# The up projection of a streaming encoder step made token-major, with 512 weight columns streamed

## The chip, the cores and the metric

The kernel runs on one core of a Trainium2 chip. The metric is device time of one execution in microseconds (us). TensorE does the matmuls, VectorE, ScalarE and GpSimd the elementwise work. SyncE, ScalarE and GpSimd issue DMAs.

## The reference, cut to what matters

One layer over 400 tokens: 16 meta tokens and 256 new frames of one stream, and 16 new frames of each of 8 running streams. Attention and mLSTM heads come first, then an output projection, then a squared-ReLU MLP, all in fp32. The meta tokens' MLP output is not wanted, so the MLP sees 384 tokens. What matters here:

```python
def merge_and_ffn(x, att, hm, og, mnorm_g, w_out, norm2_g, w_up, w_down):
    ...
    x = x + mix @ w_out                              # D_MODEL = 2048
    u = jax.nn.relu(rms_norm(x, norm2_g) @ w_up)     # D_FF = 8192
    return x + jnp.square(u) @ w_down
```

## The kernel before, in words

Each fp32 matmul is made of three on TensorE in the float32r format: both factors are split into a high part and a low part (the rest), and high x high, high x low and low x high are summed in PSUM. So each tile of weights is loaded into `raw` by SyncE, split by ScalarE into `w_hi` (`split_hi`, L494) and by VectorE into `w_lo` (`split_lo`, L503), and used. A tile is a pair of loads of 512 KB and has four quarters of 128x512. `w_hi` and `w_lo` hold four quarters: ScalarE may split a quarter of the next tile once TensorE is done with the same quarter of this one (`w_used`). ScalarE and VectorE thus run one tile ahead of TensorE, in an order that is written out in each engine's program. Every other operation of theirs stands between two splits of that order.

The MLP runs in four groups of 2048 features (`GROUPS`), each group an up stage of 16 tiles and a down stage of 16 tiles.

In the up stage the weights are stationary: a tile holds 2048 rows by 128 columns of `w_up`, and the 384 tokens (`x2g_hi`, `x2g_lo`, features on partitions) stream past (`mm_tile`, L523 to L525, 48 matmuls of 384 columns). The result in `acc[j]` has 128 features on its partitions and tokens in its columns. VectorE multiplies it by the norm's factor, which has been spread over all partitions beforehand (L1882 to L1885, `spread_rstd`), into `n_t` (L1894), and takes ReLU times itself into `n_sq` (L1898). ScalarE makes its high part `a_hi` (L1243), GpSimd its low part `a_lo` (L846).

In the down stage the activations are stationary: for each of four blocks of 512 columns, 16 k and three groups of 128 tokens, `a_hi`/`a_lo` [128 features, 128 tokens] are loaded and 512 columns of `w_down` stream past (`mm_down`, L623 to L625) into three PSUM banks. VectorE adds them to `y_rows` (L1917). The two sets of three banks take turns (`down_banks`).

Ahead of the MLP, the second half of the output projection (`mm_out`) ends each of four column blocks of the residual x2, which is token-major in `y_rows`. The first two blocks are turned to feature-major by VectorE's 32x32 block transpose (L1644), 12 stores from GpSimd that put the blocks in place in device memory, and one load (the helper at L657). The last eight tiles are turned by TensorE (L2214) into PSUM banks that `x2_bank` names. ScalarE also issues 32 stores of new keys earlier on (L1079), and SyncE loads the key cache in 128-byte pieces (L905).

## Time and profile before

| | |
|---|---|
| median of 3 runs | 1751.79 us (1751.28 to 1752.92) |
| the profiled execution | 1751.83 us |
| its span | 1750.0 us |
| TensorE busy | 1743.2 us |
| VectorE, ScalarE, GpSimd busy | 902.0, 670.9, 224.1 us |
| weight loads of w_up | 128 of 512 KB, 4.0 us to landing |
| weight loads of w_down | 128 of 512 KB, 3.7 us to landing |

The span is the time between the first and the last instruction of the profiled execution. Busy times overlap between engines. A matmul's recorded duration overlaps that of the next one, so TensorE's pace is read from the distance between starts.

### The profile page before, as it was taken

The numbers are of one execution on the slowest core, as the hardware profiler recorded it, in microseconds if no ns is written. First come the engines' busy times: TensorE is split into PE (matmuls) and PEld (weight loads), VectorE is DVE, ScalarE is ACT, GpSimd is POOL, SyncE is SP. The second block draws the span as 40 slices with busy tenths as digits, with TensorE's granted clock in tenths as the row PEclk, the third lists the DMA queues.
The fourth block names the chain that finished last, engine by engine and source line by source line (L and its number), as shares of the span: only waits on it lengthen the run. The fifth ranks groups of instructions, "written<-read, shape, count | busy, mean of one in ns | idle before, by whom it ended". The sixth has DMA issues, their size and how long they took to land.

```text
span 1750.0 us, 27145 instructions
## 1 busy us (share of the span) xinstructions
PE 1743.2 (100%) x9246; PEld 1581.0 (90%) x9246; DVE 902.0 (52%) x1724; ACT 670.9 (38%) x1256; POOL 224.1 (13%) x312
## 2 busy tenths in 40 slices
PE   9999999999999999999999999999999999999999
PEld 8999998889997789998889999888999888999887
DVE  5634776666677656554344444344454334545333
ACT  5323754444354444333333333333333333333332
POOL 3301010002351250110000110000111000111000
PEclk9999999999999999999999999999999999999999
DMA  7675469998788584444334443334443334444443
GB/s 187 186 181 150 122 169 223 204 203 215 201 259 258 147 210 123 129 122 126 127 123 129 120 125 126 124 128 121 130 121 125 126 123 130 120 127 125 142 147 97
DMA packets 382545, 264.69 MB, mean 151 GB/s; under 512 B 92860, under 2 KB 328572, under 8 KB 382476
## 3 DMA queue, kind: packets, MB, share of 16 engines
q1 hardware_dynamic: 353190, 222.09, 45.1%
q0 software_dynamic: 14224, 37.83, 8.2%
q10 hardware_dynamic: 15062, 3.86, 1.1%
q8 instruction: 42, 0.69, 0.2%
q14 instruction: 27, 0.22, 0.0%
HBM read 246.47 MB, written 23.03 MB: 154 GB/s over the span
## 4 chain that ended last, share of the span: by engine, by line
PE 98%; DVE 1%; issue 0%; ACT 0%; POOL 0%; POOLq 0%; DVEq 0%; ACTq 0%
PE acc L523 18%; PE acc L524 18%; PE acc L525 18%; PE bank L624 9%; PE bank L625 8%; PE bank L623 8%; PE bank L1940 3%; PE ssb L623 2%; PE ssb L624 2%; PE ssb L625 2%; PE ssb L1940 1%; PE bank L569 1%; PE bank L570 1%; PE bank L568 1%; PE acc L568 1%; PE acc L570 1%
## 5 line engine op out<-in xcount | busy, mean ns | idle before, releaser
L503 DVE TENSOR_TENSOR w_lo<-raw,w_hi 128x512 fp32r<-128x512 f32 x768 | 556.4, 733 | 769.2 <-ACT w_hi L494 768.3
L494 ACT ACTIVATE w_hi<-raw 128x512 fp32r<-128x512 f32 x768 | 483.5, 632 | 821.1 <-PE acc L525 400.2
L524 PE MATMUL acc<-x2g_lo,w_hi 128*128 128x384 f32 x1024 | 348.0, 340 | 0.0
L523 PE MATMUL acc<-x2g_hi,w_hi 128*128 128x384 f32 x1024 | 345.9, 338 | 0.0
L525 PE MATMUL acc<-x2g_hi,w_lo 128*128 128x384 f32 x1024 | 344.6, 337 | 0.0
L523 PE MATMUL acc<-a_hi,w_hi 128*128 128x400 f32 (+1 forms) x768 | 268.1, 349 | 0.2 <-DVE w_lo L503 0.2
L524 PE MATMUL acc<-a_lo,w_hi 128*128 128x400 f32 (+1 forms) x768 | 262.9, 342 | 0.0
L525 PE MATMUL acc<-a_hi,w_lo 128*128 128x400 f32 (+1 forms) x768 | 262.3, 342 | 0.0
L624 PE MATMUL bank<-w_lo,a_hi 128*128 128x512 f32 x640 | 253.0, 395 | 0.0
L625 PE MATMUL bank<-w_hi,a_lo 128*128 128x512 f32 x640 | 252.6, 395 | 0.0
L623 PE MATMUL bank<-w_hi,a_hi 128*128 128x512 f32 x640 | 252.0, 394 | 0.0
L525 PEld LDWEIGHTS acc<-x2g_hi,w_lo 128*128 128x128 f32 x1024 | 193.4, 189 | 0.0
L524 PEld LDWEIGHTS acc<-x2g_lo,w_hi 128*128 128x128 f32 x1024 | 192.4, 188 | 0.1
L523 PEld LDWEIGHTS acc<-x2g_hi,w_hi 128*128 128x128 f32 x1024 | 191.9, 187 | 0.5 <-DVE w_lo L503 0.3
L846 POOL TENSOR_TENSOR a_lo<-n_sq,a_hi 128x384 f32 x64 | 65.2, 1018 | 899.4 <-ACT a_hi L1243 899.4
L523 PEld LDWEIGHTS acc<-a_hi,w_hi 128*128 128x128 f32 x768 | 144.2, 188 | 6.5 <-issue 4.0
L625 PEld LDWEIGHTS bank<-w_hi,a_lo 128*128 128x128 f32 x640 | 120.7, 189 | 27.7
L624 PEld LDWEIGHTS bank<-w_lo,a_hi 128*128 128x128 f32 x640 | 120.3, 188 | 27.8
L623 PEld LDWEIGHTS bank<-w_hi,a_hi 128*128 128x128 f32 x640 | 120.4, 188 | 27.6
L525 PEld LDWEIGHTS acc<-a_hi,w_lo 128*128 128x128 f32 x768 | 144.8, 189 | 0.0
L524 PEld LDWEIGHTS acc<-a_lo,w_hi 128*128 128x128 f32 x768 | 144.3, 188 | 0.3
L1243 ACT ACTIVATE a_hi<-n_sq 128x384 f32 (+1 forms) x64 | 33.7, 527 | 131.9 <-DVE n_sq L1898 131.9
(344 smaller groups left out, 1533.9 us busy)
## 6 DMA issues: line engine op xcount, KB each, us to landing
raw<-in_w_up SPq DMA_DIRECT2D x128, 512.0 KB, 4.0
raw<-in_w_down SPq DMA_DIRECT2D x128, 512.0 KB, 3.7
raw<-in_w_in SPq DMA_DIRECT2D x94, 512.0 KB, 4.7
raw<-in_w_out SPq DMA_DIRECT2D x32, 512.0 KB, 4.9
vc<-in_cache_v POOLq DMA_DIRECT2D x32, 256.0 KB, 7.3
kc<-in_cache_k SPq DMA_DIRECT2D x128, 64.0 KB, 3.2
state_blocks<-in_state_C POOLq DMA_DIRECT2D x16, 256.0 KB, 4.5
C_blk<-state_blocks SPq DMA_DIRECT2D x4, 1024.0 KB, 8.5
```

What stands on the lines that cost most here:

```text
L494: e.activation(w_hi[:, q], raw[:, slot, 4 * (q % 2):4 * (q % 2) + 4, :], ACT.Copy).then_inc(hi_ready, 1)
L503: e.tensor_tensor(w_lo[:, q], raw[:, slot, 4 * (q % 2):4 * (q % 2) + 4, :], w_hi[:, q].bitcast(F32), ALU.subtract).then_inc(lo_ready, 1)
L523: e.matmul(out, w_hi[:, q, kk], hi[:, k, at], start=k == 0, stop=False, skip_group_check=True)
L524: e.matmul(out, w_hi[:, q, kk], lo[:, k, at], start=False, stop=False, skip_group_check=True)
L525: last = e.matmul(out, w_lo[:, q, kk], hi[:, k, at], start=False, stop=k == KT - 1, skip_group_check=True)
L568: e.matmul(out, a_hi[:, k, rows], hi_w, start=k % 8 == 0, stop=False, skip_group_check=True)
L570: last = e.matmul(out, a_lo[:, k, rows], hi_w, start=False, stop=k % 8 == 7, skip_group_check=True)
L623: e.matmul(out, a_hi[:, k, rows], hi_w, start=k == 0, stop=False, skip_group_check=True)
L624: e.matmul(out, a_hi[:, k, rows], lo_w, start=False, stop=False, skip_group_check=True)
L625: last = e.matmul(out, a_lo[:, k, rows], hi_w, start=False, stop=k == KT - 1, skip_group_check=True)
L846: e.tensor_tensor(a_lo[:, bass.ds(2 * i + j, 1), LIVE], n_sq[:, j:j + 1, LIVE], a_hi[:, bass.ds(2 * i + j, 1), LIVE].bitcast(F32), ALU.sub ...
L1940: return e.matmul(out, lhsT, rhs, start=start, stop=stop, skip_group_check=True)
```

## The change

The up projection takes down's form. For each group there are four blocks (`U_BLOCKS`) of 512 features. The normed tokens are stationary (128 at a time) and 512 columns of `w_up` stream past (`mm_up`), into the same `down_banks` in turn. SyncE loads `w_up` as it loads `w_down`, in rows of 512 columns.

The result is now token-major, and the down stage wants it with features on partitions. For each block: VectorE scales by the norm's factor, one number per partition now, and takes ReLU from PSUM into `u_rows` (`turn_u`, three operations of 128x512). ScalarE squares in place (`square_u`, three). VectorE transposes within 32x32 blocks into `u_blk` (three). ScalarE issues 12 stores of 64 KB that put the blocks in their places in device memory (`store_u`). GpSimd loads the turned block of 512 features into `u_land` (`u_part`). ScalarE makes its high part (`u_hi`, four), GpSimd its low part (four). In ScalarE's order the squares stand behind the last split of the block (fourth tile's turn), the stores behind the first split of the next block's first turn, the high parts behind the first split of its third turn; behind a group's last block these turns are those of the down stage's first block. In all there are 16 blocks.

The spreading of the norm's factor over the partitions is gone. The x2 tiles 8 to 15 that TensorE turns go into `acc` (8 to 11, 15) and the second set of down banks (12 to 14), since the first set is now up's. The semaphore `y_summed` is renamed `rows_summed` and `x2_landed` `rows_landed`, with the counts moved to suit.

```diff
@@ -189,6 +189,7 @@
 Y_STARTS = (NPR, META, META + P)
 Y_TURNS = (1, 2, 0)
 X2_BLOCKS = 2
+U_BLOCKS = 4
 Y_OUT = 2 * len(Y_PLAN)
 Y_OUT_SUMMED = 2 * 2 * 4
 LAST_IN_BANK = [("nout")] + [(x, *y, NH - 1) for x, y in (("num", (0,)), ("num", (1,)), ("num", (2,)), ("cp", ()),
@@ -290,6 +291,7 @@
         gate_rows = nc.dram_tensor("gate_rows", [3, NH, TOK], F32).ap()
         new_keys = nc.dram_tensor("new_keys", [4, 8, 13 * 32, 32], F32).ap()
         x2_turned_d = nc.dram_tensor("x2_turned", [X2_BLOCKS, 4 * P, 3 * P], F32).ap()
+        u_turned_d = nc.dram_tensor("u_turned", [2, 4 * P, 3 * P], F32).ap()
         state_blocks_d = nc.dram_tensor("state_blocks", [P, BD * NH, DV], F32).ap()
@@ -592,9 +594,56 @@
                     (T_OUT2 + 7, 1): (8, 9), (T_OUT2 + 7, 3): (10, 11)}.get((t, q), ())
         def x2_bank(k):
-            if k == KT - 1:
-                return bank[1]
-            return down_banks[k // 4 % 2][k % 4 % 3]
+            if k < 12 or k == KT - 1:
+                return acc[k % 2 if k < 12 else 0]
+            return down_banks[1][k % 4]
+        u_rows, u_blk = (m1[:].rearrange("p j t -> p (j t)")[:, 12 * P * x:12 * P * (x + 1)].rearrange("p (r n) -> p r n", r=3)
+                         for x in range(2))
+        u_land = stage[:].rearrange("p j t -> p (j t)")[:, 0:12 * P].rearrange("p (k t) -> p k t", k=4)
+        def u_store(e, g, b, r):
+            for a in range(4):
+                e.dma_start(bass.AP(tensor=u_turned_d.tensor,
+                                    offset=(b % 2) * 4 * P * 3 * P + Y_STARTS[r] - META + 32 * a,
+                                    ap=[[3 * P, 32], [32 * 3 * P, 16], [1, 32]]),
+                            u_blk[32 * a:32 * a + 32, r]).then_inc(S("u_stored"), 16)
+        def mm_up(e, g, b, first=False, after=None):
+            out = down_banks[b % 2]
+            def products(kq, q, r):
+                k = 4 * kq + q
+                if k == 0:
+                    if b < 2:
+                        e.wait_ge(S("y_added"), 12 * g + (Y_OUT - 6 + 3 * b + r + 1))
+                    else:
+                        e.wait_ge(S("u_read"), 12 * g + (3 * (b - 2) + r + 1))
+                hi_w, lo_w = (w[:, q].rearrange("p k n -> p (k n)") for w in (w_hi, w_lo))
+                to, rows = out[r][:], slice(Y_STARTS[r], Y_STARTS[r] + P)
+                e.matmul(to, x2g_hi[:, k, rows], hi_w, start=k == 0, stop=False, skip_group_check=True)
+                e.matmul(to, x2g_hi[:, k, rows], lo_w, start=False, stop=False, skip_group_check=True)
+                last = e.matmul(to, x2g_lo[:, k, rows], hi_w, start=False, stop=k == KT - 1, skip_group_check=True)
+                if k == KT - 1 and r < 2:
+                    last.then_inc(S("rows_summed"), 1)
+                if r == 2:
+                    last.then_inc(w_used, 1)
+            for kq in range(4):
+                pair, j = g * KT + (T_MLP // 2 + 2 * b + kq // 2), kq % 2
+                for qs in ((0,), (1,), (2, 3)) if kq == 3 else ((0,), (1,), (2,), (3,)):
+                    e.wait_ge(lo_ready, 8 * pair + 4 * j + qs[-1] + 1)
+                    if first:
+                        e.wait_ge(S("x2_lo_made"), 4 * kq + qs[-1] + 1)
+                    for r in range(3):
+                        for q in qs:
+                            products(kq, q, r)
+                    if after and kq == 0:
+                        for q in qs:
+                            after(q)
         x2_blocks = stage[:].rearrange("p j t -> p (j t)")[:, 0:3 * 4 * P]
...
-            e.memset(st4[:, 5], 0.0).then_inc(S("u_lo_made"), 1)
-            e.memset(st4[:, 4], 0.0).then_inc(S("u_lo_made"), 1)
-            with e.Fori(0, GROUPS) as g:
-                with e.Fori(0, KT // 2) as i:
-                    for j in range(2):
-                        e.wait_ge(S("u_hi_made"), KT * g + 2 * i + j + 1)
-                        e.tensor_tensor(a_lo[:, bass.ds(2 * i + j, 1), LIVE], n_sq[:, j:j + 1, LIVE],
-                                        a_hi[:, bass.ds(2 * i + j, 1), LIVE].bitcast(F32),
-                                        ALU.subtract).then_inc(S("u_lo_made"), 1)
+                    "rows_landed")
+            def u_part(g, b, first=False):
+                n = U_BLOCKS * g + b
+                e.wait_ge(S("u_stored"), 192 * n + 192)
+                if not first:
+                    e.wait_ge(S("u_lo_made"), 4 * n)
+                e.dma_start(u_land, u_turned_d[b % 2].rearrange("(k p) t -> p k t", p=P)).then_inc(S("rows_landed"), 16)
+                for k in range(4):
+                    e.wait_ge(S("u_hi_made"), KT * g + (4 * b + k + 1))
+                    e.tensor_tensor(a_lo[:, 4 * b + k, LIVE], u_land[:, k], a_hi[:, 4 * b + k, LIVE].bitcast(F32),
+                                    ALU.subtract).then_inc(S("u_lo_made"), 1)
+            for g in range(GROUPS):
+                for b in range(U_BLOCKS):
+                    u_part(g, b, first=g == b == 0)
             for n, (r, c) in enumerate(Y_PLAN[:-3]):
                 e.wait_ge(S("y_added"), Y_OUT + 12 * (GROUPS - 1) + n + 1)
@@ -941,9 +997,10 @@
                 if T_OUT + 2 <= t < T_OUT + 6:
                     load_x(t - T_OUT - 2)
             with e.Fori(0, GROUPS) as g:
-                with e.Fori(0, KT // 2) as i:
-                    for j in range(2):
-                        load_tile(e, g * KT + i + T_MLP // 2, j, w_up[0], 0, g * D + i * (2 * P) + P * j)
+                with e.Fori(0, U_BLOCKS) as c:
+                    for kq in range(4):
+                        load_rows(e, g * KT + 2 * c + (T_MLP // 2 + kq // 2), kq % 2, w_up[0],
+                                  kq * 4 * P, g * D + c * (4 * P))
                 with e.Fori(0, 4) as c:
                     for kq in range(4):
                         load_rows(e, g * KT + 2 * c + (T_MLP // 2 + KT // 2 + kq // 2), kq % 2, w_down[0],
@@ -1231,34 +1288,56 @@
                     e.wait_ge(S("y_logged"), 1)
                     e.activation(y_st[:, 4], y_st[:, 3], ACT.Exp, scale=-0.5).then_inc(S("y_rooted"), 1)
-            def split_up(g, first=False):
-                e.wait_ge(w_used, 4 * PER_GROUP * g + 4 * T_MLP)
-                def pair(i, after):
-                    for j in range(2):
-                        split_hi(e, g * KT + i + (T_MLP // 2 + j), 1 - j, after=after if j == 0 else None)
-                        e.wait_ge(S("u_made"), KT * g + 2 * i + j + 1)
-                        at = bass.ds(2 * i + j, 1)
-                        e.activation(a_hi[:, at, LIVE], n_sq[:, j:j + 1, LIVE], ACT.Copy).then_inc(S("u_hi_made"), 1)
-                if first:
-                    pair(0, first_up)
-                with e.Fori(1 if first else 0, KT // 2) as i:
-                    pair(i, None)
+            def square_u(g, b):
+                for r in range(3):
+                    e.wait_ge(S("u_read"), 12 * g + (3 * b + r + 1))
+                    e.activation(u_rows[:, r], u_rows[:, r], ACT.Square).then_inc(S("u_squared"), 1)
+            def store_u(g, b):
+                for r in range(3):
+                    e.wait_ge(S("u_blocks"), 12 * g + (3 * b + r + 1))
+                    u_store(e, g, b, r)
+            def u_hi(g, b):
+                e.wait_ge(S("rows_landed"), 16 * (U_BLOCKS * g + b) + 16 * (X2_BLOCKS + 1))
+                for k in range(4):
+                    e.activation(a_hi[:, 4 * b + k, LIVE], u_land[:, k], ACT.Copy).then_inc(S("u_hi_made"), 1)
+            def up_block(g, b, first=False):
+                for kq in range(4):
+                    def after(q):
+                        if first and kq == 0:
+                            first_up(q)
+                        if b and (kq, q) == (0, 0):
+                            store_u(g, b - 1)
+                        elif b and (kq, q) == (2, 0):
+                            u_hi(g, b - 1)
+                        elif b < U_BLOCKS and (kq, q) == (3, 3):
+                            square_u(g, b)
+                    split_hi(e, g * KT + (T_MLP // 2 + 2 * b + (kq + 1) // 2), (kq + 1) % 2, after=after)
             def split_down(g):
-                with e.Fori(0, KT // 2) as i:
+                up_block(g, U_BLOCKS)
+                with e.Fori(2, KT // 2) as i:
                     for j in range(2):
                         split_hi(e, g * KT + i + (T_MLP // 2 + KT // 2 + j), 1 - j)
+            def split_up(g, first=False):
+                for b in range(U_BLOCKS):
+                    up_block(g, b, first=first and b == 0)
             split_up(0, first=True)
             split_down(0)
-            with e.Fori(1, GROUPS - 1) as g:
+            for g in range(1, GROUPS - 1):
                 split_up(g)
                 split_down(g)
             split_up(GROUPS - 1)
-            with e.Fori((T_END - KT) // 2, T_END // 2 - 1) as p:
+            up_block(GROUPS - 1, U_BLOCKS)
+            with e.Fori((T_END - KT) // 2 + 2, T_END // 2 - 1) as p:
                 for j in range(2):
                     split_hi(e, p + j, 1 - j)
             split_hi(e, T_END // 2 - 1, 1)
@@ -1878,30 +1957,32 @@
                     y_step(tt(y_st[:, 5], y_st[:, 5], y_st[:, 2], ALU.mult), 4)
                     y_step(ts(y_st[:, 5], y_st[:, 5], -0.5, 1.5, ALU.mult, ALU.add), 5)
                     y_step(tt(y_st[:, 6], y_st[:, 5], y_st[:, 4], ALU.mult), 6)
-                    for r in range(3):
-                        last = ts(n_y[:, 0, r * P:(r + 1) * P], ident[:], y_st[:, 6, r:r + 1], None, ALU.mult)
-                    last.then_inc(S("y_diag_made"), 1)
-                    e.wait_ge(S("rstd2_spread"), 1)
-                    e.tensor_copy(rstd_x[:, LIVE], bank[0][:, LIVE]).then_inc(S("rstd2_ready"), 1)
-                    e.wait_ge(S("rstd2_ready"), 1)
+            def turn_u(g, b):
+                n = U_BLOCKS * g + b
+                for r in range(3):
+                    if r < 2:
+                        e.wait_ge(S("rows_summed"), 16 * g + (Y_OUT_SUMMED + 2 * b + r + 1))
+                    else:
+                        tile_done(e, g * KT + (T_MLP // 2 + 2 * b + 1), 1)
+                    ts(u_rows[:, r], down_banks[b % 2][r][:], y_st[:, 6, r:r + 1], 0.0, ALU.mult,
+                       ALU.max).then_inc(S("u_read"), 1)
+                for r in range(3):
+                    e.wait_ge(S("u_squared"), 12 * g + (3 * b + r + 1))
+                    if r == 0 and not (isinstance(n, int) and n == 0):
+                        e.wait_ge(S("rows_landed"), 16 * n + 16 * X2_BLOCKS)
+                    e.transpose(u_blk[:, r], u_rows[:, r]).then_inc(S("u_blocks"), 1)
             def up(g, first=False):
-                def pair(i, after):
-                    for j in range(2):
-                        t = KT * g + 2 * i + j
-                        split_lo(e, g * KT + i + (T_MLP // 2 + j), 1 - j, after=after if j == 0 else None)
-                        tile_done(e, g * KT + i + T_MLP // 2, j)
-                        tt(n_t[:, LIVE], acc[j][:, LIVE], rstd_x[:, LIVE], ALU.mult).then_inc(acc_free, 1)
-                        e.wait_ge(acc_free, KT * g + 2 * i + (T_OUT + j + 1))
-                        e.wait_ge(S("u_lo_made"), t + 1)
-                        stt(n_sq[:, j, LIVE], n_t[:, LIVE], 0.0, n_t[:, LIVE], ALU.max,
-                            ALU.mult).then_inc(S("u_made"), 1)
-                if first:
-                    pair(0, first_up)
-                with e.Fori(1 if first else 0, KT // 2) as i:
-                    pair(i, None)
+                for b in range(U_BLOCKS):
+                    for kq in range(4):
+                        def after(q):
+                            if first and b == 0 and kq == 0:
+                                first_up(q)
+                            if (kq, q) == (3, 3):
+                                turn_u(g, b)
+                        split_lo(e, g * KT + (T_MLP // 2 + 2 * b + (kq + 1) // 2), (kq + 1) % 2, after=after)
             def down(g, c2, half, last):
                 for kq in range(4):
...
@@ -2218,35 +2299,20 @@
             for t in range(T_OUT2, T_MLP):
                 mm_out(e, t, after=new_x)
-            def spread_rstd(q):
-                if q == 1:
-                    e.wait_ge(S("y_diag_made"), 1)
-                    for r in range(3):
-                        last = mm(bank[0][:, Y_STARTS[r]:Y_STARTS[r] + P], ones[:], n_y[:, 0, r * P:(r + 1) * P], True, True)
-                    last.then_inc(S("rstd2_spread"), 1)
-            x2_there = lambda k: e.wait_ge(S("x2_lo_made"), k + 1)
-            def up_pair(g, i, afters=(None, None), first=False):
-                for j in range(2):
-                    mm_tile(e, g * KT + i + T_MLP // 2, j, x2g_hi, x2g_lo, each=x2_there if first and j == 0 else None,
-                            at=LIVE, after=afters[j], used=KT * g + 2 * i + (T_OUT + j))
             def down_all(g):
                 with e.Fori(0, 2) as c2:
                     for half in range(2):
                         mm_down(e, g, c2, half)
-            up_pair(0, 0, (lambda q: new_x(T_MLP, q), spread_rstd), first=True)
-            with e.Fori(1, KT // 2) as i:
-                up_pair(0, i)
+            for b in range(U_BLOCKS):
+                mm_up(e, 0, b, first=b == 0, after=(lambda q: new_x(T_MLP, q)) if b == 0 else None)
             down_all(0)
             with e.Fori(1, GROUPS - 1) as g:
-                with e.Fori(0, KT // 2) as i:
-                    up_pair(g, i)
+                for b in range(U_BLOCKS):
+                    mm_up(e, g, b)
                 down_all(g)
-            with e.Fori(0, KT // 2) as i:
-                up_pair(GROUPS - 1, i)
+            for b in range(U_BLOCKS):
+                mm_up(e, GROUPS - 1, b)
             for c2 in range(2):
                 for half in range(2):
                     mm_down(e, GROUPS - 1, c2, half, tail=c2 == 1 and half == 1)
```

## Rows read from the trace of the kernel before

**Rows 1.** The page's chain that ended last, share of the span by engine.

```profile
PE 98%; DVE 1%; issue 0%; ACT 0%; POOL 0%; POOLq 0%; DVEq 0%; ACTq 0%
```

**Rows 2.** Busy time by stretch: start:end us, busy us by engine, PEclk, DMA share, GB/s.

```profile
940.20:1075.20 135.00, 135.00 (x769) 135.00 (x767) 67.81 (x97) 47.48 (x79) 15.29 (x15) 1.00 0.42 124
1075.20:1208.90 133.70, 133.70 (x578) 108.58 (x578) 50.83 (x75) 41.03 (x65) 1.02 (x1) 1.00 0.39 125
```

**Rows 3.** Waits from 640 on, ScalarE's and SyncE's: us in all, times, longest.

```profile
ACT w_hi L494 <- PE acc L525: 225.6, 193, 1.5
...
SPq L471 <- DVE w_lo L503: 451.9, 128, 6.6
```

**Rows 4.** TensorE's timeline (start us, us, instruction), first matmul of six stages.

```profile
669.01 0.42 PE L523 MATMUL acc<-x2g_hi,w_hi 128*128 128x384 f32 x1
...
806.58 0.39 PE L623 MATMUL bank<-w_hi,a_hi 128*128 128x512 f32 x1
...
940.12 0.34 PE L523 MATMUL acc<-x2g_hi,w_hi 128*128 128x384 f32 x1
...
1075.37 0.39 PE L623 MATMUL bank<-w_hi,a_hi 128*128 128x512 f32 x1
...
1208.90 0.34 PE L523 MATMUL acc<-x2g_hi,w_hi 128*128 128x384 f32 x1
...
1344.15 0.39 PE L623 MATMUL bank<-w_hi,a_hi 128*128 128x512 f32 x1
```

**Rows 5.** TensorE's timeline, turns of x2 tiles in the first up tile.

```profile
673.31 0.82 PE L2214 MATMUL bank<-ident,y_rows 128*128 128x128 f32 x6
673.96 0.49 PE L2214 MATMUL ssb<-ident,y_rows 128*128 128x128 f32 x3
```

**Rows 6.** Timeline of ScalarE and VectorE behind the border at 1344.15.

```profile
1344.41 0.63 ACT L494 ACTIVATE w_hi<-raw 128x512 fp32r<-128x512 f32 x1 [1.54 <-PE acc L525]
...
1345.08 0.69 DVE L503 TENSOR_TENSOR w_lo<-raw,w_hi 128x512 fp32r<-128x512 f32 x1 [1.48 <-ACT w_hi L494]
1345.69 0.55 DVE L1894 TENSOR_TENSOR n_t<-acc,rstd_x 128x384 f32<-128x384 f32 x1
```

**Rows 7.** Timeline of VectorE and ScalarE, operations of one kind in a row.

```profile
619.25 1.88 DVE L1631 TENSOR_TENSOR y_rows<-bank,y_rows 128x512 f32<-128x512 f32 x3
621.26 1.90 DVE L1644 STREAM_TRANSPOSE stage<-y_rows 128x512 f32<-128x512 f32 x3
...
686.15 1.66 ACT L494 ACTIVATE w_hi<-raw 128x512 fp32r<-128x512 f32 x3
```

**Rows 8.** Timeline of DMA issues (q), ScalarE's first and last at the start among them.

```profile
253.24 0.35 ACTq L1079 DMA_DIRECT2D new_keys<-ko  x1
253.69 0.64 ACT L494 ACTIVATE w_hi<-raw 128x512 fp32r<-128x512 f32 x1 [2.88 <-DVE ko L1564]
...
0.78 0.42 ACTq L964 DMA_DIRECT2D g_rows<-in_norm_g  x1
...
6.27 0.88 ACTq L969 DMA_DIRECT2D xn<-in_x_prompt  x1
...
249.91 6.06 SPq L905 DMA_DIRECT2D kc<-in_cache_k  x8
```

**Rows 9.** All stores of line 1079: ns of an issue (min/median/max), landing.

```profile
L1079 ACTq DMA_DIRECT2D new_keys<-ko x32: 309/310/1100, 253.2 to 338.4; - x32
...
DMA to landing us min/median/max: 2.0/4.2/10.0
```

**Rows 10.** Timeline of GpSimd and ScalarE, second x2 block through device memory.

```profile
640.12 7.74 POOL L657 DMA_DIRECT2D x_turned<-stage  x12 [4.60 <-DVE stage L1644]
652.16 0.78 POOL L657 DMA_DIRECT2D m<-x_turned  x1 [4.29 <-DMA x_turned<-stage]
...
657.24 1.13 ACT L1215 ACTIVATE x2g_hi<-m,g 128x384 fp32r<-128x384 f32 x2 [0.38 <-DMA m<-x_turned]
```

**Rows 11.** The page's costliest groups: busy us, mean ns, idle before.

```profile
L846 POOL TENSOR_TENSOR a_lo<-n_sq,a_hi 128x384 f32 x64 | 65.2, 1018 | 899.4 <-ACT a_hi L1243 899.4
```

More of the change, by code:

```diff
@@ L571, in products @@
                 if k % 8 == 7 and r < 2:
-                    last.then_inc(S("y_summed"), 1)
+                    last.then_inc(S("rows_summed"), 1)
                 if r == 2:
@@ new lines, in u_store @@
+        def u_store(e, g, b, r):
[19 more added lines that the diff above has]
+                if k == KT - 1 and r < 2:
+                    last.then_inc(S("rows_summed"), 1)
+                if r == 2:
[12 more added lines that the diff above has]
+                            after(q)
@@ L609, in x2_there_for @@
             if k < 4 * X2_BLOCKS:
-                e.wait_ge(S("x2_landed"), 16 * (k // 4 + 1))
+                e.wait_ge(S("rows_landed"), 16 * (k // 4 + 1))
             else:
@@ L620, in products @@
                     e.wait_ge(S("y_added"), 12 * g + 6 * c2 + (Y_OUT - 6 + 3 * half + r + 1))
+                    e.wait_ge(S("u_read"), 12 * g + (6 + 3 * half + r + 1))
                 hi_w, lo_w = (w[:, q].rearrange("p k n -> p (k n)") for w in (w_hi, w_lo))
@@ L626, in products @@
                 if k == KT - 1 and r < 2:
-                    last.then_inc(S("y_summed"), 1)
+                    last.then_inc(S("rows_summed"), 1)
                 if r == 2:
@@ L634, in mm_down @@
                     e.wait_ge(lo_ready, 8 * pair + 4 * j + qs[-1] + 1)
-                    e.wait_ge(S("u_lo_made"), KT * g + (4 * kq + qs[-1] + 3))
+                    e.wait_ge(S("u_lo_made"), KT * g + (4 * kq + qs[-1] + 1))
                     for r in range(3):
@@ L837, in _ @@
                 dma(m1[:, 4 * c:4 * c + 4, 0:3 * P], x2_turned_d[c].rearrange("(k p) t -> p k t", p=P),
-                    "x2_landed")
-            e.memset(st4[:, 5], 0.0).then_inc(S("u_lo_made"), 1)
-            e.memset(st4[:, 4], 0.0).then_inc(S("u_lo_made"), 1)
-            with e.Fori(0, GROUPS) as g:
-                with e.Fori(0, KT // 2) as i:
-                    for j in range(2):
-                        e.wait_ge(S("u_hi_made"), KT * g + 2 * i + j + 1)
-                        e.tensor_tensor(a_lo[:, bass.ds(2 * i + j, 1), LIVE], n_sq[:, j:j + 1, LIVE],
-                                        a_hi[:, bass.ds(2 * i + j, 1), LIVE].bitcast(F32),
-                                        ALU.subtract).then_inc(S("u_lo_made"), 1)
+                    "rows_landed")
[12 more added lines that the diff above has]
+                    u_part(g, b, first=g == b == 0)
             for n, (r, c) in enumerate(Y_PLAN[:-3]):
@@ L1626, in add_out @@
                     if r < 2:
-                        e.wait_ge(S("y_summed"), 2 * (4 * half + c) + r + 1)
+                        e.wait_ge(S("rows_summed"), 2 * (4 * half + c) + r + 1)
                     else:
@@ L1912, in down @@
                     if r < 2:
-                        e.wait_ge(S("y_summed"), 8 * g + 4 * c2 + (Y_OUT_SUMMED + 2 * half + r + 1))
+                        e.wait_ge(S("rows_summed"), 16 * g + 4 * c2 + (Y_OUT_SUMMED + 8 + 2 * half + r + 1))
                     else:
@@ L2210, in new_x @@
                     e.wait_ge(S("y_added"), Y_OUT // 2 + 3 * (k // 4) + 3)
-                    if k % 4 == 3:
-                        e.wait_ge(S("x2_lo_made"), k - 2 if k < KT - 1 else 12)
+                    if k in (10, 11, KT - 1):
+                        e.wait_ge(S("x2_lo_made"), k - 1 if k < KT - 1 else 11)
                     for r in range(3):
```

## The prediction

> **What bounds the kernel now.** I read the chain of waits first, then the busy times in stretches, then TensorE's timeline at the borders of the stages. TensorE holds 98% of the chain [rows 1]: only what TensorE does, or waits for, moves the end. In the two stages of the MLP (up projection, then down projection, four groups of each) it never pauses, and the granted clock is 1.00, its upper level of 2.4 GHz [rows 2]. Its weight loads are busy for all 135.00 us of an up stage, but for 108.58 of 133.70 in a down stage. ScalarE and VectorE are ahead of TensorE by design: ScalarE waits 225.6 us in all for TensorE to give back a quarter of `w_hi`, and SyncE waits 451.9 us for a free `raw` buffer before it may issue an up load [rows 3]. So the weight traffic has slack, and the question for the change is the pace of TensorE's new instructions on one side, and whether ScalarE and VectorE stay ahead on the other.
>
> **TensorE's pace.** A whole up stage runs from 940.12 to 1075.37, 135.25 us for 768 matmuls of 384 columns (0.1761 from start to start) [rows 4]. The down stage behind it runs to 1208.90, 133.53 us for 576 matmuls of 512 columns (0.2318). The changed up stage has 4 blocks x 16 k x 3 row groups x 3 products = 576 matmuls of down's form: the same columns in fewer instructions. I take down's 133.53 us for it: 1.72 us less in each of three groups, 5.2 us (the other two groups repeat the pair of intervals to 0.01 us). Group 0 lasts from 669.01 to 806.58, 137.57 us. In it stay the twelve turns of the last x2 tiles, of which six took 673.96 - 673.31 = 0.65 us [rows 5], so 1.3 for twelve; what goes is the spreading of the norm's factor over all partitions (three fp32 products, three VectorE scalings, a copy). 137.57 - 133.53 - 1.3 = 2.7 us. TensorE's part is -7.9 us. Where no engine falls behind, the span is 1742.1. Bounds of this term: without the group 0 part -5.2, and down's pace is measured, so not much beyond -8.
>
> The Trainium skill, TensorE: Matmul & The Clock Gate, section "Back-to-back issue gap", gives an isolated warm gap of N/2.4 + 2.5 ns. As an estimate by that formula 3072 x 162.5 ns against 2304 x 215.8 ns would save 2.0 us over the four groups, where the trace's own paces save 6.9 (5.2 plus 1.7 in group 0): rows decide.
>
> **Work that lies beside it.** Down's blocks have 64 quarters, 133.53/64 = 2.09 us each; one tile of four quarters is 8.35 us, and a block of four tiles 33.4 us. Per up block VectorE gets 3 scalings from PSUM and 3 block transposes of 128x512, ScalarE 3 squares and 4 copies, GpSimd one load and 4 subtractions. Before, four 128-feature tiles cost VectorE eight operations and ScalarE four copies; the sums of both engines (67.8 and 47.5 of 135 us, [rows 2]) leave room. What matters is when they come, since `w_hi` and `w_lo` hold one tile of four quarters and every split is queued behind them.
>
> I set t = 0 at the start of TensorE's first matmul of the next block, and take the border at 1344.15 [rows 4]. ScalarE's last split of the finished block's turn starts at 0.26, VectorE's at 0.93, and VectorE is free at 1.54 [rows 6]. The three scalings start at 1.54, 2.14, 2.74 (three adds from PSUM took 1.88 together, each 0.60 behind the last, [rows 7]). The squares follow each at once: from 2.26, 2.90 and 3.46. ScalarE's split of quarter 0 of the next tile follows at 4.0, 0.53 behind the last square (three splits in 1.66, [rows 7]). The transposes start at 3.34 and follow 0.62 apart (three in 1.90, [rows 7]); the first is ready at 4.01, the third at 5.24. TensorE needs quarter 0 at 8.35, and VectorE does its low part right behind the transposes, by 6: covered.
>
> **The twelve stores are not covered.** Behind quarter 0 ScalarE's queue issues the block's 12 stores (3 row groups x 4 partition groups, 64 KB each in 512 pieces of 128 bytes), and only then splits quarter 1. ScalarE does not compute past a DMA that it issues: the issue at 253.24 took 0.35, and the activation behind it starts at 253.69, 0.10 after it ended [rows 8]. With p us from one issue to the next, they run from 4.05 to 4.05 + 12p. Then come 0.10, and the 1.36 us from the start of a split to the end of its low part (1344.41 to 1345.77, [rows 6]). TensorE wants that quarter at 8.35 + 2.09 = 10.43. So it stops for s = 4.05 + 12p + 1.46 - 10.43 = 12p - 4.92 us in each block, and the point from which the stores cost anything is p = 0.41.
>
> What is p? A lone store of nearly this form from ScalarE (52 KB in 128-byte pieces) took 0.31, median of 32 [rows 9]. Behind one another they have no row on this queue in this form. The nearest: ScalarE's 11 loads at the start run from 0.78 to 7.15, 0.58 each; SyncE's loads of 64 KB in 128-byte pieces, the same count of pieces, took 6.06 us for 8, 0.76 each, behind weight loads in their own queue [rows 8]. The ends are 0.31 (s = 0) and 0.76 (s = 4.2). I take 0.58, the one row of back-to-back issues on ScalarE's own queue, where no weight load is ahead; s = 2.0 us. There are 16 blocks, the last of each group too, whose stores fall into the down stage: +32.6 us. Behind the stop ScalarE catches up at once, 0.53 per split against 2.09 per quarter, so each block pays once.
>
> In a sentence apart: the Trainium skill, DMA: Bandwidth & Descriptors, section "Issuing engines are not separate DMA queues", says that the time to start a DMA on a sequencer is "usually small relative to the DMA itself". Applied here it speaks for the lone-store row of 0.31 and for no stop, the first rival below. The trace agrees that it is small beside a landing (0.31 against 4.2, [rows 9]), but small is not free when 12 stand in one row.
>
> **The way through device memory.** Last issue at 4.05 + 7.0 = 11.0. In the stage before the MLP the same twelve pieces from GpSimd's queue were issued until 647.86, the load of them began at 652.16 (4.30 later), its issue took 0.78, and its data was used at 657.24, 4.3 after that [rows 10]. Here: 11.0 + 4.3 + 0.8 + 4.3 = 20.4. ScalarE asks for it behind the split of quarter 0 of the fourth tile, which TensorE frees at 2 x 8.35 + 2.09 + s + 0.26 = 21.1: no wait. After the four copies (taken as 0.53 each, like the splits) and 1.46 as above, quarter 1 must be ready by 3 x 8.35 + 2.09 + s = 29.2, so the landing may come as late as 29.2 - 2.1 - 1.46 = 25.6, 5.2 later than worked out. The low parts (4 x 1.02 on GpSimd, [rows 11]) are needed from tile 4 of down's first block, at 25.0 + s; the first is there by 23.2: hidden by the three tiles ahead of them. Each block's traffic (0.79 MB out in 6144 pieces, 0.79 MB back) goes into DMA engines that are 39 to 42% busy [rows 2], and the up loads change to 2 KB pieces like down's: no cost taken for either.
>
> The renamed semaphores, the new PSUM buffers for x2 tiles 8 to 15 and their waits, and the reading waits of the down banks come long after their releases (TensorE turned the x2 tiles into idle banks at 673.31 without a pause behind them, [rows 5]): nothing, and a few tenths once if wrong. The tail is not touched.
>
> **Sum.** 1750.0 - 7.9 + 32.6 = 1774.7 span. The profiled execution took 1751.83 for a span of 1750.0, so 1.8 lies around it, and it stands 0.04 from the median of 1751.79: 1776.5 us.
>
> **Rivals.**
> *Issues stay cheap.* p below 0.41, no stop: 1742.1 + 1.8 = 1743.9, faster by 0.45%. For it: 0.31 per lone store, and this queue is empty when the stores begin. Against it: every run of issues in the trace, on both queues, is above 0.41 on average.
> *Both effects nearly cancel.* p of 0.43 to 0.49, a stop of 0.2 to 1.0: 1748 to 1759, the lower half within the bound. For it: the shorter ones among ScalarE's first issues (0.42, [rows 8]).
> *The landing is the late one.* If the stores, sharing the 16 engines with the weight stream, need the worst landing of a store from this queue (10.0 instead of 4.2, [rows 9]), the data comes at 26.2 and costs 0.6 more per block, 1786; if the load is late by as much again, it comes at 32.0 and costs 6.4 more per block, 1879. Against it: the x2 case ran in a busier stretch. It decides from a landing 5.2 us later than mine.
> *A deeper stop.* p at or above SyncE's 0.76: s of 4.2 or more, 1811 and up.
>
> **Chances.** Forecast (p of 0.50 to 0.76, 1761 to 1811, its own range) 0.60; cheap issues 0.20; cancelling 0.09; late landing 0.06; deeper stop 0.05. What a measurement tells from no change is about 0.2%, 3.5 us. Faster: the cheap case and a part of the cancelling one, 0.23. Same 0.07, slower 0.70. The range reaches from the cheap case to the top of the forecast's own, 1744 to 1811.
>
> **What would show it.** Right: 576 matmuls per up stage 0.232 apart; a TensorE pause in quarter 1 of the second tile behind every up block, ended by VectorE's low part behind ScalarE's split, with ScalarE idle before that split for the length of 12 issues; nothing lost at the fourth tile. Wrong: issues of 0.35 in a row and a chain with no pause (first rival); ScalarE waiting on the landed data with TensorE stopped near the fourth tile (third); a granted clock below 1.00 behind the pauses, which would make every matmul after them dearer; or up matmuls that don't keep down's pace.

## The result, and the profile after

The changed kernel takes 1782.15 us (median of 6 runs, 1780.23 to 1783.34), the one before 1752.09 (6 runs, 1751.28 to 1752.92): a ratio of 1.0171, 95% interval [1.0158, 1.0184], so 1.7% slower. The profiled execution took 1781.35 us with a span of 1779.2. Forecast were 1776.5 us and slower.

The page's first line on busy time and its chain by engine, of the kernel after:

```profile
PE 1742.8 (98%) x8472; PEld 1474.4 (83%) x8472; DVE 875.1 (49%) x1688; ACT 688.6 (39%) x1304; POOL 242.4 (14%) x326
...
PE 87%; ACTq 5%; DVE 4%; ACT 2%; issue 2%; DMA 0%; DVEq 0%
```

Against [rows 1] TensorE's share of the chain falls from 98 to 87%, and ScalarE's queue (ACTq), which was at 0, holds 5%: DMA issues are now on the path that sets the end. The DVE, ACT and issue shares belong to the same stretches, as the chain walks back over the late split, the squares and the scalings.

The busy times by stretch of the kernel after, one row for the up stage of group 1 and one for the down stage behind it (columns as in [rows 2], the stretch cut at the stages' first matmuls):

```profile
946.80:1088.50 141.70, 135.57 (x577) 109.23 (x576) 58.13 (x84) 49.20 (x85) 15.74 (x15) 0.99 0.54 152
1088.50:1224.30 135.80, 134.03 (x577) 108.17 (x577) 54.35 (x80) 43.75 (x73) 5.26 (x5) 1.00 0.45 137
```

The up stage has down's 576 matmuls and its weight loads are busy for 109 us of it instead of 135, but it takes 141.7 us instead of 135.0, and TensorE is busy for 135.57 of them. The down stage takes 2.1 us more than before: the last block's stores fall into it.

One block border in time, group 1, ScalarE's timeline (start, us, engine, line, times, idle before). TensorE's first matmul of the new block starts at 980.10.

```profile
979.67 1.33 ACT L496 ACTIVATE w_hi<-raw 128x512 fp32r<-128x512 f32 x2 [2.84 <-PE bank L629]
982.42 1.95 ACT L1295 ACTIVATE m<-m 128x512 f32<-128x512 f32 x3 [1.42 <-DVE m L1969]
984.27 0.62 ACT L496 ACTIVATE w_hi<-raw 128x512 fp32r<-128x512 f32 x1
984.35 6.41 ACTq L608 DMA_DIRECT2D u_turned<-m  x12
990.86 2.19 ACT L496 ACTIVATE w_hi<-raw 128x512 fp32r<-128x512 f32 x4 [5.97 <-PE ssb L629]
```

The squares (L1295), the split of quarter 0, twelve issues that take 6.41 us, and only then the splits that had been due. The "5.97 <-PE" is an example of a wait put down to the wrong one: TensorE had given the quarter back at about 984.5, and what ended at 990.76 was the last issue. VectorE's and then TensorE's timeline of the same stretch:

```profile
981.64 2.06 DVE L1969 TENSOR_SCALAR m<-bank,y_st 128x512 f32<-128x512 f32 x3
983.62 1.88 DVE L1975 STREAM_TRANSPOSE m<-m 128x512 f32<-128x512 f32 x3
...
991.52 1.90 DVE L505 TENSOR_TENSOR w_lo<-raw,w_hi 128x512 fp32r<-128x512 f32 x3 [5.44 <-ACT w_hi L496]
```

```profile
990.29 0.39 PE L629 MATMUL ssb<-w_hi,x2g_lo 128*128 128x512 f32 x1
992.27 0.50 PE L627 MATMUL bank<-w_hi,x2g_hi 128*128 128x512 f32 x1 [1.59 <-DVE w_lo L505]
992.60 0.39 PE L628 MATMUL bank<-w_lo,x2g_hi 128*128 128x512 f32 x1
```

From 990.29 to 992.27 are 1.98 us where 0.23 is the pace: a stop of 1.75 us. The matmul after that starts 0.33 later and not 0.23; behind each of the other stops it is the same. There are 16 such stops, one per block. By the starts of the matmuls on both sides they come to 31.8 us: twelve of 1.68 to 1.89, and 2.12, 2.64, 2.74 and 2.95. The view of waits (us in all, times, longest) has them as 12 in up and 4 in down:

```profile
PE bank L627 <- DVE w_lo L505: 22.9, 12, 2.8
PE bank L673 <- DVE w_lo L505: 6.3, 4, 1.6
```

(It counts from the recorded end of the matmul before, which lies 0.16 us into the pause, so 29.2 and not 31.8.)

The stores and the load of the turned block, page of the kernel after, section on DMA issues (us to landing last), and the stores' line (ns of one issue, min/median/max):

```profile
u_turned<-m ACTq DMA_DIRECT2D x192, 64.0 KB, 1.9
stage<-u_turned POOLq DMA_DIRECT2D x16, 768.0 KB, 6.8
```

```profile
L608 ACTq DMA_DIRECT2D u_turned<-m x192: 309/522/1528, 707.4 to 1650.3; - x192
```

### The profile page after: what moved, and what is told of

It is laid out like the page before. It is cut to its first block, busy times and chain, and to the rows that moved or that the text cites. A ratio compares the mean times of both kernels' runs of the same rounds, so it can differ in the third digit from the quotient of the medians.

```text
span 1779.2 us, 24776 instructions
## 1 busy us (share of the span) xinstructions
PE 1742.8 (98%) x8472; PEld 1474.4 (83%) x8472; DVE 875.1 (49%) x1688; ACT 688.6 (39%) x1304; POOL 242.4 (14%) x326
## 4 chain that ended last, share of the span: by engine, by line
PE 87%; ACTq 5%; DVE 4%; ACT 2%; issue 2%; DMA 0%; DVEq 0%
PE bank L673 8%; PE bank L674 8%; PE bank L675 8%; PE acc L525 8%; PE acc L526 8%; PE acc L527 8%; PE bank L627 7%; PE bank L628 6%; PE bank L629 6%; ACTq L608 5%; PE bank L2021 3%; ACT w_hi L496 2%; PE ssb L673 2%; PE ssb L674 2%; PE ssb L675 2%
## 5 line engine op out<-in xcount | busy, mean ns | idle before, releaser
L505 DVE TENSOR_TENSOR w_lo<-raw,w_hi 128x512 fp32r<-128x512 f32 x768 | 537.2, 706 | 834.2 <-ACT w_hi L496 833.5
L496 ACT ACTIVATE w_hi<-raw 128x512 fp32r<-128x512 f32 x768 | 476.9, 629 | 940.9 <-PE ssb L675 180.4
L627 PE MATMUL bank<-w_hi,x2g_hi 128*128 128x512 f32 x640 | 255.0, 398 | 23.1 <-DVE w_lo L505 22.9
L628 PE MATMUL bank<-w_lo,x2g_hi 128*128 128x512 f32 x640 | 253.8, 397 | 0.0
L629 PE MATMUL bank<-w_hi,x2g_lo 128*128 128x512 f32 x640 | 253.4, 396 | 0.0
L627 PEld LDWEIGHTS bank<-w_hi,x2g_hi 128*128 128x128 f32 x640 | 121.2, 189 | 55.9 <-DVE w_lo L505 28.1
L629 PEld LDWEIGHTS bank<-w_hi,x2g_lo 128*128 128x128 f32 x640 | 121.4, 190 | 28.2
L628 PEld LDWEIGHTS bank<-w_lo,x2g_hi 128*128 128x128 f32 x640 | 121.1, 189 | 27.1
L896 POOL DMA_DIRECT2D stage<-u_turned x16 | 12.2, 763 | 784.2 <-DMA u_turned<-m 784.2
L899 POOL TENSOR_TENSOR a_lo<-stage,a_hi 128x384 fp32r<-128x384 f32 x64 | 71.8, 1150 | 146.1 <-ACT a_hi L1307 146.1
```

Of the source, the lines that this page charges most:

```text
L496: e.activation(w_hi[:, q], raw[:, slot, 4 * (q % 2):4 * (q % 2) + 4, :], ACT.Copy).then_inc(hi_ready, 1)
L505: e.tensor_tensor(w_lo[:, q], raw[:, slot, 4 * (q % 2):4 * (q % 2) + 4, :], w_hi[:, q].bitcast(F32), ALU.subtract).then_inc(lo_ready, 1)
L627: e.matmul(to, x2g_hi[:, k, rows], hi_w, start=k == 0, stop=False, skip_group_check=True)
L628: e.matmul(to, x2g_hi[:, k, rows], lo_w, start=False, stop=False, skip_group_check=True)
L629: last = e.matmul(to, x2g_lo[:, k, rows], hi_w, start=False, stop=k == KT - 1, skip_group_check=True)
```

## The experiments

Three theories stood against each other. A: ScalarE's queue is held by the twelve issues. B: the traffic through device memory, or its landing, stops TensorE. C: the block's extra work on VectorE and ScalarE is late by itself.

**The stores on SyncE** (`stores_on_sync`). SyncE's loops over groups and blocks are written out, and ScalarE's call is gone (the two places that matter):

```diff
+                        if c and kq == 2:
+                            store_u(g, c - 1)          # SyncE, behind the load of the third tile
...
-                        if b and (kq, q) == (0, 0):
-                            store_u(g, b - 1)          # ScalarE
```

> The same 12 stores per block, issued by SyncE behind its load of the next block's third tile instead of by ScalarE. Theory A (ScalarE's queue is held by the 12 issues, 0.53 us each in the trace of the changed kernel, so quarter 1 of the next turn is late): no stop of TensorE, span 1742 to 1743, time 1743 to 1746. Theory B (the traffic of the stores and the load through device memory, or its landing, is what stops TensorE): the traffic is the same, so the stops stay, 1775 to 1785. Theory C (the block's extra work on VectorE and ScalarE, three scalings, three squares, three transposes in front of the next splits, is late by itself): stops of some tenths at quarter 0 or 1 stay, 1750 to 1765.

Measured: 1743.22 us (5 runs), ratio to the kernel before 0.9954 [0.994, 0.9968], span 1741.3. TensorE never stops. Its stretches of up in group 1 and of down behind it, and one block's stores on SyncE's queue with the loads behind them:

```profile
937.00:1070.30 133.30, 133.30 (x578) 108.36 (x577) 58.83 (x84) 50.26 (x85) 16.43 (x15) 1.00 0.57 162
1070.30:1203.80 133.50, 133.50 (x577) 108.24 (x576) 54.57 (x80) 43.85 (x72) 5.27 (x5) 1.00 0.46 138
```

```profile
1041.21 6.36 SPq L608 DMA_DIRECT2D u_turned<-m  x12
1047.63 1.00 SPq L482 DMA_DIRECT2D raw<-in_w_up  x2
```

The same twelve issues take the same 6.36 us there, and the same bytes move, yet all 16 stops are gone. B and C fall: the same traffic and the same work on VectorE and ScalarE cost TensorE nothing. SyncE can afford the 6.36 us: `raw` holds two tiles, and in this variant SyncE still waits 784.8 us in all for a free part of it (218 times, from 690 on).

**Four stores behind each of three quarters** (`stores_spread`). All twelve stay on ScalarE (the lines that decide):

```diff
-                        if b and (kq, q) == (0, 0):
-                            store_u(g, b - 1)
+                        if b and kq == 0 and q < 3:
+                            store_u(g, b - 1, q)       # row group q's four
```

> The 12 stores stay on ScalarE, but four each behind the splits of quarters 0, 1 and 2 instead of all behind quarter 0. Theory A: four issues are 2.1 us, about what TensorE needs for a quarter (2.09), and quarter 1 is ready at 4.25 + 2.1 + 1.5 = 7.9 against 10.4, so no stop, 1743 to 1747. Theory B: same traffic, 1775 to 1785, or worse, as the last store is issued 1.5 us later. Theory C: 1750 to 1765.

Measured: 1745.88 us (6 runs), ratio 0.9967 [0.9955, 0.9979], span 1744.5. The stops at quarter 1 of the second tile are gone. So twelve issues on ScalarE are affordable; twelve in a row are not. Of the 3.2 us over the first variant's span 1.3 lie at 644.5, before the MLP and its first store. The other 1.9 are one stop of 0.68 us, one of 0.32 and a few of 0.1 to 0.2. The two larger ones have another cause. They lie in the fourth tile and show the prediction's third rival, the late landing, at a small scale:

```profile
746.81 4.36 ACTq L608 DMA_DIRECT2D u_turned<-m  x4
762.25 1.77 ACT L1306 ACTIVATE a_hi<-stage 128x384 fp32r<-128x384 f32 x4 [4.36 <-DMA stage<-u_turned]
764.57 4.90 DVE L505 TENSOR_TENSOR w_lo<-raw,w_hi 128x512 fp32r<-128x512 f32 x5 [5.96 <-ACT w_hi L496]
768.32 0.50 PE L627 MATMUL bank<-w_hi,x2g_hi 128*128 128x512 f32 x1 [0.52 <-DVE w_lo L505]
```

The last four of the twelve issues take 4.36 us here and not 2.1, as the twelfth alone takes 2.62; in 14 of the 16 blocks it takes 1.28 to 2.62 us, and why is open. The block lands later for it, ScalarE's copies start 24.0 us behind the border at 738.26, and the splits behind them are late; two of VectorE's low parts also take 1.5 us each instead of 0.7. The other block with such a stop (0.32) has them at 23.4; in the remaining 14 they start by 22.8.

**The stores on GpSimd** (`stores_on_gpsimd`), ahead of its load of the turned block; ScalarE's call is gone, as in the first variant:

```diff
                 n = U_BLOCKS * g + b
+                for r in range(3):
+                    e.wait_ge(S("u_blocks"), 12 * g + (3 * b + r + 1))
+                    u_store(e, g, b, r)                # GpSimd
                 e.wait_ge(S("u_stored"), 192 * n + 192)
```

> The 12 stores issued by GpSimd ahead of its load of the turned block, 0.65 us each as in the stage before the MLP. Theory A: no stop at the second tile; the block lands later (4.0 + 7.8 + 4.3 + 0.8 + 6 = 23), close to the 23.6 by which the high parts must be begun, so 1743 to 1750. Theory B: 1775 to 1785. Theory C: 1750 to 1765.

Measured: 1743.24 us (4 runs), ratio 0.9953 [0.9938, 0.9968], span 1741.0, no stop, although an issue costs 0.654 us there and ScalarE now waits for the landed block in each of the 16 (36.1 us in all, the longest 2.7). That wait stays inside the margin that the prediction worked out: its copies start 21.2 to 22.4 us behind the border, and the bound was 25.6 with a stop of 2.0, so 23.6 without one. The two blocks of the spread variant that stopped had them at 23.4 and 24.0, so the bound holds to some tenths.

**Large pieces** (`large_pieces`). Same count of stores and bytes on ScalarE, 32 pieces of 2048 bytes instead of 512 of 128. It leaves out the turning of the block, so its result is not the layer's:

```diff
-                                    ap=[[3 * P, 32], [32 * 3 * P, 16], [1, 32]]),
+                                    ap=[[4 * P, 32], [1, 4 * P]]),
```

> Twelve stores per block on ScalarE as in the changed kernel, but each writes its 64 KB in 32 pieces of 2048 bytes to a contiguous place instead of 512 pieces of 128 bytes: the block is not turned in device memory, so the activations of the down projection are in a wrong order. Theory A with a price per DMA: issues stay at 0.50 to 0.55 us, the stop stays near 1.8 to 2.0 us per block, 1776 to 1784. Theory A with a price per piece: issues fall toward 0.31, stops vanish, 1743 to 1746. Theory B: traffic is far cheaper for the engines, stops shrink, under 1760.

Measured: 1764.36 us (4 runs), ratio 1.0073 [1.0057, 1.0088], between the two expectations. ScalarE's timeline at the border in group 1, and the stores' line:

```profile
981.06 5.60 ACTq L608 DMA_DIRECT2D u_turned<-m  x12
986.76 2.19 ACT L496 ACTIVATE w_hi<-raw 128x512 fp32r<-128x512 f32 x4 [5.16 <-issue]
```

```profile
L608 ACTq DMA_DIRECT2D u_turned<-m x192: 308/446/1237, 707.6 to 1633.2; - x192
```

With a sixteenth of the pieces twelve issues fall from 6.41 to 5.60 us. Most of the price is per DMA. The stop falls by the same 0.8 us, from 1.75 to 0.95 in that block. Over all 16 blocks the issues take 14.0 us less (85.6 instead of 99.7) and the stops come to 14.0 us less (17.8 instead of 31.8): what the issues save passes to TensorE one for one.

**Eight on ScalarE** (`eight_on_scalar`). The third row group's four go to SyncE, in the place they had in the first variant:

```diff
-                for r in range(3):                     # ScalarE's store_u
+                for r in range(2):
...
+                for r in (2,):                         # SyncE's store_u
```

> Eight of the 12 stores stay on ScalarE behind quarter 0, the four of the third row group go to SyncE. Theory A with the measured 0.535 us per issue: the stop of a block is 1.75 + 0.535 x (n - 12) us for n issues on ScalarE, so -0.4 for 8: no stop, span 1741 to 1743, 1743 to 1746. A rival, that the stop comes from having any stores on ScalarE's queue (a drain or a hand-over in front of the next activation, whatever their number): stops of 1 us or more stay, above 1760.

Measured: 1745.52 us (5 runs), ratio 0.9962 [0.9948, 0.9976], span 1742.4; two stops, 0.53 and 0.43 us, in 16 blocks. They fit theory A too. A usual row of eight takes 4.25 us, 2.2 less than twelve, which leaves 0.4 us to spare; in these two blocks one issue of the row took 1.38 and 1.27 us, and the rows 5.18 and 5.09. The rival falls: 14 blocks with stores on ScalarE's queue have no stop above 0.3 us.

**Sixteen on ScalarE** (`sixteen_on_scalar`). GpSimd waits for the four extra stores too before it loads the block (the new issues alone are shown):

```diff
+            if r == 2:
+                for a in range(4):
+                    e.dma_start(...u_twice_d..., u_blk[32 * a:32 * a + 32, r]).then_inc(S("u_twice"), 16)
```

> Sixteen stores on ScalarE per block: the third row group's four are issued a second time, to a second buffer that nothing reads. Theory A: 1.75 + 0.535 x 4 = 3.9 us per block, 62 us in 16 blocks over the span of 1741.3 without stops, 1805, and 1.5 us more for each stop behind which TensorE's clock is granted at half: 1807 to 1830. The rival (price does not hang on the number): near the changed kernel's 1782. On the clock: if stops of 2 us and more bring the half clock, nearly all 16 stops now do, and the time is near 1830; if only some do by chance, it is nearer to 1810.

Measured: 1843.7 us (4 runs), ratio 1.0524 [1.0508, 1.054], span 1840.8. The 16 stops are 3.94 to 5.29 us, twelve of them between 3.94 and 4.05: the expected 3.9. They add up to 66.5 us. The rest, 33 us, is nearly all the clock: 1.5 us per stop had been expected and 2.1 were paid, so the time lies above the expected 1807 to 1830. The group 1 stretches of up and down (PEclk is the third figure from the right), and a stretch of 4 us that starts 0.4 us after one of its stops has ended:

```profile
961.90:1114.10 152.20, 140.15 (x577) 112.70 (x577) 58.23 (x84) 49.20 (x85) 15.79 (x15) 0.94 0.54 147
1114.10:1253.30 139.20, 135.36 (x578) 109.50 (x577) 54.37 (x80) 43.66 (x72) 5.27 (x5) 0.99 0.45 135
...
1129.00:1133.00 4.00, 4.00 (x13) 3.12 (x13) 1.26 (x3) 0.73 (x2) 0.69 (x1) 0.63 0.77 225
```

Behind each of its 16 stops matmuls run 0.43 us apart instead of 0.23 for a while.

Stops against the number of issues in a row on ScalarE: 8: none but two small ones; 12: 1.75; 16: 4.0. The slope from 12 to 16 is 0.56 us per issue, the measured time from one issue to the next 0.53; the rows themselves grow from 6.4 to 8.65 us.

## Why the prediction was right

**TensorE's pace.** Forecast -7.9 us. The variant with no stop shows it alone: 133.3 us per up stage against 135.25, and 134.7 in group 0 against 137.57; 3 x 1.95 + 2.9 = 8.7, and its span is 8.7 below 1750.0. The term was 0.8 too small, since 512-column matmuls on the normed tokens run 0.2314 apart, a trifle faster than down's.

**The way to the stop.** The step that decided, twelve issues in front of quarter 1's split, is in the trace as worked out. Its pieces from the border at 980.10: VectorE free at 1.54 (worked out 1.54), first store at 4.25 (4.05, the scalings take 0.66 each from one to the next and not 0.60), last issue done at 10.66 (11.0), quarter 1's low part ready and TensorE going at 12.17, against 10.42 when it wanted it. The price from one issue to the next was 0.534 and not 0.58, which takes 0.55 us off the stop, and the later start gives back only 0.20: 1.75 for this stop, 1.78 for the mean of the twelve usual ones, against 2.04. Sixteen of these would be 28.5 us. That all 16 come to 31.8, so near the forecast 32.6, is luck: four longer ones, for which the prediction had no reason, add 3.3.

**The four longer stops.** In three of them (2.64, 2.74, 2.95) one of the twelve issues took 1.44 to 1.53 us instead of 0.5. Each of these three issues meets a transfer of 16 KB on queue 8, which the page lists as kind "instruction", and no other row of the kernel has one that starts within it. The DMA view of 1019.8 to 1021.5, the time of the second one (packets, MB, share of 16 engines):

```profile
q8 instruction: 1, 0.02, 3.3%
```

The other variants agree. In the large-piece variant (1.24, 1.20, 0.91 in the same blocks), with eight and with sixteen issues, three such transfers each start within a row on ScalarE, and with the stores on SyncE five; each time an issue that overlaps the transfer takes 0.9 to 2.1 us. On GpSimd six start within rows, and no issue is longer than 0.69. So the long issue comes with the transfer and not with the stores' bytes; that the transfer is its cause is not tested. The 2.12 has normal issues, but its next split starts 0.39 us behind the last of them and not 0.10. The 2.95 has such a delay too, 0.38, besides its long issue. What these 0.3 us are stays open.

**The landing.** The late landing, third rival, did not come in the changed kernel (the spread variant shows it, twice): the load of group 1's first turned block is issued at 992.44, such a load lands in 6.8 us (median of 16), and ScalarE's four copies follow its split without a wait:

```profile
1000.98 0.63 ACT L496 ACTIVATE w_hi<-raw 128x512 fp32r<-128x512 f32 x1 [1.46 <-PE ssb L629]
1001.52 1.75 ACT L1307 ACTIVATE a_hi<-stage 128x384 fp32r<-128x384 f32 x4
```

The stores landed faster than the x2 block's (1.7 us from the last issue to the load, against 4.3), the load slower (6.8 against 5.1), and so the block is there at about 19.1 and not at 20.4; ScalarE asks for it at 21.4. The two errors partly cancel.

**The cheap issues.** The first issue of every row of twelve takes 0.309 us, as the lone stores of [rows 9] had, and those behind it 0.50 to 0.54, but for a few. So the price of a lone store is not that of a row, and ScalarE's loads at the start came nearest to it: 0.58 against 0.53 measured. That of SyncE's key loads, 0.76 in [rows 8], was put down to the weight loads ahead of them in the queue; the first variant's stores stand behind weight loads in the same queue and took 0.53 each, so this reading does not hold, and what made the key loads dearer is not shown. Beside this stands what the Trainium skill, DMA: Bandwidth & Descriptors, section "Issuing engines are not separate DMA queues", says: issuing from another engine only saves the sequencer's time to start a DMA. The trace agrees (6.41 us on ScalarE, 6.36 on SyncE for the same twelve), and in this kernel the loss came from that time alone: with the same traffic, but the stores on SyncE, it is gone. Beside the 1.9 us to landing, 0.53 us is not small.

**What the sum left out: the clock.** The prediction named a granted clock below 1.00 among what would prove it wrong, and gave it no price. TensorE's starts behind the longest stop, kernel after, and the clock of 4 us of it:

```profile
783.79 0.39 PE L629 MATMUL ssb<-w_hi,x2g_lo 128*128 128x512 f32 x1
786.97 0.50 PE L627 MATMUL bank<-w_hi,x2g_hi 128*128 128x512 f32 x1 [2.79 <-DVE w_lo L505]
...
788.06 0.63 PE L628 MATMUL bank<-w_lo,x2g_hi 128*128 128x512 f32 x1
788.49 0.63 PE L629 MATMUL bank<-w_hi,x2g_lo 128*128 128x512 f32 x1
```

```profile
787.00:791.00 4.00, 4.00 (x11) 3.13 (x12) 1.72 (x3) 1.26 (x3) 0.65 (x1) 0.61 0.68 209
```

Eight matmuls 0.43 us apart: the lower level of 1.2 GHz for this stretch, 1.5 us dearer. It happened behind three of the 16 stops (2.95, 2.12, 2.64), 4.6 us in all, in no other place of the MLP, and nowhere in the variants without stops, whose granted clock is 1.00 throughout. With it the sum closes to 1.5 us: 1741.3 + 31.8 + 4.6 = 1777.7 against 1779.2. The matmul behind each stop that starts 0.33 and not 0.23 later makes 1.6 us in 16.

So the mechanism was right in each step, and the sizes less so: the span was forecast 4.5 us too low (1774.7 against 1779.2). TensorE's pace and the stops' lengths were each forecast 0.8 us too dear, the second by luck; the clock (4.6) and the slow second matmul (1.6), at nothing in the sum, are what it lacked. The forecast time lies 5.6 us below the median, as this kernel's median lies 0.8 above its profiled execution, and 2.2 us and not 1.8 lie around that one's span.

## What to carry to other kernels

An engine that stands in a lockstep with TensorE pays for each DMA that it issues, 0.31 us alone and 0.53 in a row here (now and then 1 to 2.6), however well the transfer itself is hidden. Count the issues that stand between two of its due operations, compare them with its lead, and give a row of stores to a queue that has only loads to issue, or spread it over several steps, and in that case look again at when the data lands. The gain of a change in instruction form can be real (8.7 us here) and hidden under stops that cost nearly four times as much; a variant that moves only the suspect shows both at once, and here gives the kernel that beats both: 1743.2 us, 0.5% under the one before.

## What was not expected of the hardware

A pause of TensorE can cost more than its length. Behind all 16 stops of 3.9 us and more the granted clock fell to half for a while, 2.1 us more per stop on average (33 us in 16), behind three of the four between 2.1 and 3.0 us in the changed kernel, and behind one of 1.99 in the large-piece variant; behind the twelve of 1.68 to 1.89 it stayed at 1.00. Why the stop of 2.74 us had none is open. And going from 512 pieces to 32 for the same 64 KB saved an eighth of a row's issue time only (6.41 to 5.60 us).

A DMA issue on ScalarE or SyncE that met a 16 KB transfer of kind "instruction" took 0.9 to 2.1 us instead of 0.5, in every row in which one started; one on GpSimd did not.
